# Forgetting attention: how the rows of maxima, the turned values, the keys' low parts and the gates' sum are made

## What is computed

```python
q, k, v, g, f_logit = jnp.split(h @ w_in, [1024, 2048, 3072, 4096], axis=-1)
log_f = jax.nn.log_sigmoid(f_logit + b_f)              # (S, 16)
qh, kh, vh = rms_norm(heads(q), q_gain), rms_norm(heads(k), k_gain), heads(v)
c = jnp.cumsum(log_f, axis=-1)                          # per head, over positions
logits = qh @ kh.T * scale + c[t] - c[s]                # causal: s <= t
o = softmax(logits) @ vh
out = (o * jax.nn.silu(g)) @ w_out
```

## Time and profile before

| | us |
|---|---|
| median of 3 runs (2279.71 to 2282.96) | 2281.61 |
| the profiled execution | 2281.86 |
| its span, first to last instruction | 2279.7 |
| PE busy in the span (96%) | 2180.8 |
| DVE busy (53%) | 1209.2 |
| ACT busy (38%) | 860.2 |
| POOL busy (24%) | 546.3 |

### The profile page before, as it was taken

How to read it: one execution, slowest core, us unless ns; L and a number is a source line. 1 busy time by engine, 2 the same in 40 slices (tenths; PEclk the granted TensorE clock), 3 DMA queues, 4 the chain that set the end, 5 groups by cost and what they waited for, 6 DMA issues and landing times.

```text
span 2279.7 us, 29292 instructions
## 1 busy us (share of the span) xinstructions
PE 2180.8 (96%) x11216; PEld 1847.7 (81%) x11216; DVE 1209.2 (53%) x1583; ACT 860.2 (38%) x1351; POOL 546.3 (24%) x292
## 2 busy tenths in 40 slices
PE   4899999999999899999899999999999999999997
PEld 4678888988888788898878877888888888878886
DVE  6963332352442634334254464566666666676745
ACT  3135554211012343323222234445546546544322
POOL 1322222333332122213223222211111111110520
PEclk9999999999999899999999999999999999999998
DMA  8112112111441211001141122111111111012201
GB/s 344 56 47 74 66 64 75 65 37 55 158 157 37 93 39 54 29 28 47 38 148 47 37 93 75 34 51 37 46 51 38 40 55 46 28 46 93 93 19 74
DMA packets 37814, 154.61 MB, mean 68 GB/s; under 512 B 4289, under 2 KB 4289, under 8 KB 36962
## 3 DMA queue, kind: packets, MB, share of 16 engines
q1 hardware_dynamic: 24992, 93.52, 11.6%
q10 hardware_dynamic: 12738, 59.87, 7.5%
HBM read 128.15 MB, written 21.04 MB: 65 GB/s over the span
## 4 chain that ended last, share of the span: by engine, by line
PE 85%; DVE 9%; issue 3%; ACT 2%; DMA 0%; DVEq 0%; SPq 0%; ACTq 0%
PE psG L322 22%; PE psG L323 21%; PE psG L324 21%; PE psA L2377 2%; PE psA L2359 2%; PE psA L2358 2%; PE psA L2375 2%; PE psA L2374 1%; PE psA L2231 1%; PE psA L322 1%; PE psA L2333 1%; PE psA L324 1%; PE psA L323 1%; DVE M L1044 1%; PE psA L422 1%
## 5 line engine op out<-in xcount | busy, mean ns | idle before, releaser
L322 PE MATMUL psG<-AH,WH 128*128 128x512 f32 x2092 | 849.5, 406 | 34.0 <-DVE AL L1000 12.2
L324 PE MATMUL psG<-AH,WL 128*128 128x512 f32 x2092 | 822.9, 393 | 0.0
L323 PE MATMUL psG<-AL,WH 128*128 128x512 f32 x2092 | 822.8, 393 | 0.0
L309 POOL TENSOR_SCALAR WH<-RAW 128x1024 fp32r<-128x1024 f32 x144 | 165.6, 1150 | 1655.7 <-PE psG L322 1148.8
L322 PEld LDWEIGHTS psG<-AH,WH 128*128 128x128 f32 x2092 | 397.6, 190 | 115.0 <-issue 23.0
L324 PEld LDWEIGHTS psG<-AH,WL 128*128 128x128 f32 x2092 | 396.6, 190 | 87.5
L323 PEld LDWEIGHTS psG<-AL,WH 128*128 128x128 f32 x2092 | 398.7, 191 | 67.6
L311 POOL TENSOR_TENSOR WL<-RAW,WH 128x1024 fp32r<-128x1024 f32 x144 | 380.8, 2645 | 12.0
L2658 DVE TENSOR_TENSOR FTL<-psA,FTH 128x512 fp32r<-128x512 f32 x192 | 106.9, 557 | 117.1 <-ACT FTH L2533 113.4
L2526 ACT ACTIVATE psA<-psA,PB 128x512 f32<-128x512 f32 x192 | 106.3, 553 | 90.4 <-PE psA L2361 53.4
L2668 DVE RECIPROCAL FDR<-psA 64x128 f32<-64x128 f32 x128 | 118.5, 941 | 33.8 <-PE psA L2377 30.9
(11 more groups left out here) (376 smaller groups left out, 3088.2 us busy)
## 6 DMA issues: line engine op xcount, KB each, us to landing
RAW<-w_tiles SPq DMA_DIRECT2D x144, 512.0 KB, 3.5
gates<-SIG ACTq DMA_DIRECT2D x16, 512.0 KB, 2.9
park<-X ACTq DMA_DIRECT2D x2, 4096.0 KB, 11.1
CB<-fox_c ACTq DMA_DIRECT2D x16, 512.0 KB, 4.3
X<-xT SPq DMA_DIRECT2D x4, 1024.0 KB, 12.1
WADA_SCALE<-w_ada SPq DMA_DIRECT2D x1, 4096.0 KB, 23.2
WADA_SHIFT<-w_ada SPq DMA_DIRECT2D x1, 4096.0 KB, 33.5
WADA_GATE<-w_ada ACTq DMA_DIRECT2D x1, 4096.0 KB, 16.4
```

Source lines behind the costliest of these rows:

```text
L309: nc.gpsimd.tensor_scalar(WH[:, i, :], RAW[:, i % RAW_SLOTS, :], 1.0, 0.0, ALU.mult, ALU.add).then_inc(w_high, 1)
L322: first = nc.tensor.matmul(out, wh, xh, start=start, stop=False)
L323: nc.tensor.matmul(out, wh, xl, start=False, stop=False)
L324: return first, nc.tensor.matmul(out, wl, xh, start=False, stop=stop)
```

## The change

1. **Gates.** LFT is laid out head by head (16 heads x 8 blocks = 128 columns), so that one matmul with `causal_sum` sums all blocks within themselves: 128 rows (head, block) by 128 positions. CF is now 128x128. Its last column times a new constant matrix `carry_sum` gives each row the total of the earlier blocks of its head; ACT adds it as a bias. One transpose of CF takes the place of eight, and the store to fox_c is 128 rows of 128. NCT and PB change their layout with it.
2. **First keys by halves.** The LO half of pair 0's key tile runs right behind the LO loop, in bank 3 of psA, and its HI half behind the HI loop, in bank 2. `pe_hi_sums` now stands behind the whole LO loop, `pe_hi_spread` behind the key's chunk 3. ACT takes the keys' raw values out of psA in four instructions of 512 columns, and does so behind the copy of the gates' sum.
3. **Maxima as eight rows.** `row(r)` is one transpose of NMX's eight columns into 8 rows of 128 (bank 3). ACT makes eight copies of 8x128, the n-th with column n of the identity as scale, so that row n keeps only its own block and the others become zero; FKB has eight rows of -1 (`max_rows`) that add them up. On ACT `row(1)` moves behind `high(1)`.
4. **Values behind row 6.** The first head's scores use the halves of psA in the other order, so pair(0) is free after row 6. The values are turned there, ahead of `row(0)`, in PE's order and in ACT's. Score 4 of the second head, no longer score 0, waits for ACT's `row(0)`.
5. **Keys' low parts among short rows.** `dve_fox_k` makes one half of one head: behind rows 1 and 2 of the first head, and behind rows 0 and 2 of the second. `turned(0)` waits for four of them.
6. The fill lists move one cut from the pieces to the maxima; the sums stay.

The layouts, `act_fox_raw` (taken out, now inline), the declarations and the memset of `max_rows` are left out here.

```diff
@@ -2098,9 +2100,9 @@
     SUMS_AT = HALF - 4 * NB
-    FILL_MAX = [0, 1, 1, 1, 1, 1, 1, 1, 2, 0, 1, 2, 1, 1, 1, 1, 1, 1, 2]
-    FILL_SUM = [3, 1, 1, 1, 1, 1, 1, 2, 1, 1, 1, 1, 2, 1, 1, 1, 1, 1, 1, 1, 1, 1, 1, 1]
-    FILL_MAX_LAST = [0, 0, 0, 0, 0, 0, 1, 1, 2, 0, 1, 2, 2, 1, 1, 2, 2, 2, 2]
+    FILL_MAX = [0, 1, 1, 1, 1, 1, 1, 1, 1, 2, 1, 2, 1, 1, 1, 1, 1, 1, 2]
+    FILL_SUM = [2, 1, 1, 1, 1, 1, 1, 2, 1, 1, 1, 1, 2, 1, 1, 1, 1, 1, 1, 1, 1, 1, 1, 1]
+    FILL_MAX_LAST = [0, 0, 0, 0, 0, 0, 1, 1, 1, 1, 1, 2, 2, 1, 1, 2, 2, 2, 2]
     FILL_SUM_LAST = [3, 1, 1, 1, 1, 1, 1, 1, 1, 1, 1, 1, 1, 1, 1, 1, 1, 1, 1, 1, 1, 1, 1, 1]
     def filled(n):
...
@@ -2154,8 +2156,8 @@
     def other_rows(r):
         return head_rows(1 - r)
-    def max_row(r):
-        return slice(64 * (1 - r), 64 * (1 - r) + 1)
+    def max_rows(r):
+        return slice(64 * (1 - r), 64 * (1 - r) + NB)
     def piece(j):
...
@@ -2268,11 +2270,17 @@
                         f.then_inc(tile_begun, 1)
                     if h and n == KC + lag - 1:
                         l.then_inc(psum_full, 1)
-                if h == 0 and n == 3:
-                    pe_hi_sums(pe, 4)
-                elif h == 0 and n == 6:
+
+            if h == 0:
+                pe_hi_sums(pe, 4)
+                pe.wait_ge(w_split, T_FOX + 2)
+            for c in range(KC):
+                f, l = half_cut(psA[:, 3 - h, :], (T_FOX + 1) % 4, c, cols)
+                if h == 0 and c == 3:
                     pe_hi_spread(pe, 4)
-        gemm(pe, *fox_tile(0, 1))
+                elif h and c == 0:
+                    f.then_inc(tile_begun, 1)
+        l.then_inc(psum_full, 1)
         pe.wait_ge(f_ready, 1)
         for n in range(NB):
...
@@ -2280,23 +2288,18 @@
                                     mat("ident")[0:FOX_HEADS, 0:FOX_HEADS])
         l.then_inc(f_turned, 1)
         pe.wait_ge(f_ready, 2)
-        for n in range(NB):
-            for m in range(n + 1):
-                l = nc.tensor.matmul(psA[0:FOX_HEADS, 2 + n // 4, (n % 4) * P:(n % 4 + 1) * P], LFT[:, m, :],
-                                     mat("causal_sum" if m == n else "ones"), start=(m == 0), stop=(m == n))
-        l.then_inc(f_turned, 1)
+        nc.tensor.matmul(psA[:, 1, 0:P], LFT[:, :, :].rearrange("p h n -> p (h n)"), mat("causal_sum"), start=True, stop=True).then_inc(f_turned, 1)
         v, gate = list(gemm_slices(pe, *fox_tile(0, 2))), list(gemm_slices(pe, *fox_tile(0, 3)))
         pe_fox_sums(pe, 0, 0)
-        for cut in v[:4]:
-            cut()
-        pe_fox_sums(pe, 0, 1)
-        for cut in v[4:6]:
+        for cut in v[:3]:
             cut()
         pe.wait_ge(f_high, 1)
-        for n in range(NB):
-            l = nc.tensor.transpose(psA[:, 2, n * FOX_HEADS:(n + 1) * FOX_HEADS], CF[0:FOX_HEADS, n * P:(n + 1) * P],
-                                    mat("ident")[0:FOX_HEADS, 0:FOX_HEADS])
-        l.then_inc(f_turned, 1)
+        nc.tensor.matmul(psA[:, 1, P:P + 1], mat("carry_sum"), CF[:, P - 1:P], start=True, stop=True).then_inc(f_turned, 1)
+        pe_fox_sums(pe, 0, 1)
+        for cut in v[3:6]:
+            cut()
+        pe.wait_ge(f_high, 2)
+        nc.tensor.transpose(psA[:, 2, 0:P], CF[:, :], mat("ident")).then_inc(f_turned, 1)
         pe_fox_spread(pe, 0, 0)
         for cut in v[6:12]:
             cut()
...
@@ -2338,10 +2341,7 @@
         def row(r):
             pe.wait_ge(fmax_ready, p * N_S + NB * (r + 1))
-            for n in range(NB):
-                l = nc.tensor.transpose(psA[:, 2 + n // 4, (n % 4) * P:(n % 4 + 1) * P],
-                                        NMX[:, r * NB + n:r * NB + n + 1].to_broadcast([P, P]), mat("ident"))
-            l.then_inc(fm_full, 1)
+            nc.tensor.transpose(psA[0:NB, 3, HALF - P:HALF], NMX[:, r * NB:(r + 1) * NB], mat("ident")).then_inc(fm_full, 1)
         def turned(j):
...
@@ -2381,27 +2381,28 @@
             if i == 0:
                 pe.wait_ge(fqk_ready, p * 2 + 1)
                 pe.wait_ge(fdup_ready, p * 2 + 1)
-            elif i == 1:
-                pe.wait_ge(fn_done, p * 2 + 2)
-            else:
+            elif i >= 2:
                 pe.wait_ge(fmax_ready, p * N_S + (i - 1))
-            score(i, 0, (i + 1) % 2)
+            score(i, 0, i % 2)
         fill(fill_max[NB])
-        row(0)
+        pe.wait_ge(fmax_ready, p * N_S + (NB - 1))
         pe.wait_ge(psum_free, p * 4 + (U_FOX + 3))
         for n in range(NB):
             l = nc.tensor.transpose(psA[:, n // 4, (n % 4) * P:(n % 4 + 1) * P], VF[:, n * P:(n + 1) * P], mat("ident"))
         l.then_inc(fv_turned, 1)
+        fill(fill_max[NB + 1])
+        row(0)
         for i in range(NB):
             fill(fill_max[NB + 2 + i])
             if i == 0:
                 pe.wait_ge(fqk_ready, p * 2 + 2)
                 pe.wait_ge(fdup_ready, p * 2 + 2)
-                pe.wait_ge(fm_ready, p * 2 + 1)
             elif i == 1:
                 pe.wait_ge(fv_ready, p + 1)
             else:
                 pe.wait_ge(fmax_ready, p * N_S + (NB + i - 1))
+            if i == 4:
+                pe.wait_ge(fm_ready, p * 2 + 1)
             score(i, 1, (i + 1) % 2)
         fill(fill_max[2 * NB + 2])
         row(1)
...
@@ -2497,15 +2492,26 @@
         nc.scalar.activation(EXF[fs, :], EXF[fs, :], ACT.Ln, bias=mat("ones")[fs, 0:1]).then_inc(f_log, 1)
         nc.scalar.activation(FHIDE[:, :], HIDE[:, 2, :].bitcast(F32), ACT.Copy, scale=-1.0)
         act.wait_ge(f_turned, 1)
-        act_fox_raw(act, 0, 0)
-        act_fox_raw(act, 0, 1)
+        act.wait_ge(psum_full, U_FOX + 1)
+        nc.scalar.activation(FSQ[0][:, :], fox_buf(0), ACT.Square).then_inc(fsq_ready, 1)
+        nc.scalar.activation(FN[0], fox_buf(0), ACT.Copy).then_inc(psum_free, 1)
         act.wait_ge(f_turned, 2)
-        nc.scalar.activation(CF[fs, :], pair(1)[fs, :], ACT.Copy).then_inc(f_high, 1)
-        act.wait_ge(f_high, 1)
-        act.dma_start(fox_c, CF[fs, :]).then_inc(c_stored, 16)
+        nc.scalar.activation(CF[:, :], psA[:, 1, 0:P], ACT.Copy).then_inc(f_high, 1)
+        act.wait_ge(psum_full, U_FOX + 2)
+        for h, cols in enumerate((LO, HI)):
+            l = nc.scalar.activation(FSQ[1][:, cols], psA[:, 3 - h, :], ACT.Square)
+        l.then_inc(fsq_ready, 1)
+        for h, cols in enumerate((LO, HI)):
+            l = nc.scalar.activation(FN[1][:, cols], psA[:, 3 - h, :], ACT.Copy)
+        l.then_inc(psum_free, 1)
+        act.wait_ge(f_turned, 3)
+        alink(nc.scalar.activation(CARRY[:, :], psA[:, 1, P:P + 1], ACT.Copy))
+        nc.scalar.activation(CF[:, :], CF[:, :], ACT.Identity, bias=CARRY[:, :]).then_inc(f_high, 1)
+        act.wait_ge(f_high, 2)
+        act.dma_start(fox_c.rearrange("h (n t) -> (h n) t", t=P), CF[:, :]).then_inc(c_stored, 16)
         act_fox_root(act, 0)
-        act.wait_ge(f_turned, 3)
-        nc.scalar.activation(NCT[:, :, :].rearrange("p n h -> p (n h)"), psA[:, 2, 0:NB * FOX_HEADS], ACT.Copy, scale=-1.0).then_inc(nct_ready, 1)
+        act.wait_ge(f_turned, 4)
+        nc.scalar.activation(NCT[:, :, :].rearrange("p h n -> p (h n)"), psA[:, 2, 0:NB * FOX_HEADS], ACT.Copy, scale=-1.0).then_inc(nct_ready, 1)
         act.wait_ge(c_stored, 16)
         for r in range(2):
             act_fox_c(act, 0, r)
...
@@ -2518,12 +2524,14 @@
         def row(r):
             act.wait_ge(fm_full, p * 2 + (r + 1))
-            nc.scalar.activation(FX2[max_row(r), r, :], pair(1)[max_row(r), :], ACT.Copy).then_inc(fm_ready, 1)
+            for n in range(NB):
+                l = nc.scalar.activation(FX2[max_rows(r), r, n * P:(n + 1) * P], psA[0:NB, 3, HALF - P:HALF], ACT.Copy, scale=mat("ident")[0:NB, n:n + 1])
+            l.then_inc(fm_ready, 1)
         def exp(j):
             r, h, n, lo, w = piece(j)
             act.wait_ge(ft_full, p * N_P + (j + 1))
-            nc.scalar.activation(psA[:, j % 2, 0:w], psA[:, j % 2, 0:w], ACT.Exp, bias=PB[:, n, r:r + 1], scale=-1.0).then_inc(fexp_done, 1)
+            nc.scalar.activation(psA[:, j % 2, 0:w], psA[:, j % 2, 0:w], ACT.Exp, bias=PB[:, r, n:n + 1], scale=-1.0).then_inc(fexp_done, 1)
         def high(j):
             r, h, n, lo, w = piece(j)
...
@@ -2543,18 +2551,19 @@
         if not more:
             act_fill(act, 7, Y[:, 2, :], (fo_read, 12), 2)
             act_fill(act, 7, Y[:, 3, :], (fo_read, 16), 3)
-        row(0)
         act.wait_ge(fv_turned, p + 1)
         for r in range(2):
             l = nc.scalar.activation(FVH[:, :, 2 * HD * r:2 * HD * r + HD], pair(0).rearrange("p (n f) -> p n f", f=P)[:, :, HD * r:HD * r + HD], ACT.Copy)
         l.then_inc(fv_high, 1)
+        row(0)
         if not more:
             for j in range(4, N_FOX_CUT):
                 act_fill(act, 7, Y[:, j, :], (fo_read, 4 * (j + 1)), j)
-        row(1)
         for j in range(N_P):
             exp(j)
             high(j)
+            if j == 1:
+                row(1)
             for x, at in enumerate((Q_AT, K_AT)):
                 if more and j in at:
```

(23 more changed lines are left out.)

18 lines of the change are left out of this document (7 added, 11 removed).

## The result

| | before | after |
|---|---|---|
| median of 5 runs | 2280.64 | 2264.55 us (2261.95 to 2269.72) |
| profiled execution, span | 2281.86, 2279.7 | 2264.58, 2262.8 |
| PE busy | 2180.8 | 2165.4 |

The ratio is 0.9928 (95% interval 0.9913 to 0.9943): faster by 0.7%, 16 us where 25.5 were forecast; 2264.55 lies inside the range of 2246 to 2270, 8.5 above the forecast of 2256.

The account below looks back on a forecast made before the run. PE bounds the kernel, busy 82.98 of each pair's 83.6 us, with longer waits in the join. Gains of 13.2 (join), 8.8 (seven looped pairs) and 3.5 (last pair) sum to 25.5 us: forecast 2256, range 2246 to 2270.

Parts of the forecast that it names:

- The hole: Join: closing PE's 4.98 us stand before the sums brings the gates' transposes 6.4 us earlier, with 1.8 new idle.
- One matmul for 36: Join, sum of the gates: 36 matmuls taking 8.03 us become one of 0.22; sums of squares start 13.7 earlier altogether.
- The clock in the join: Join: the new 1.8 us idle may drop the clock, costing up to 1.7 us; 0.5 taken.
- Removed from a pass: Each looped pair: 1.46 us of transposes removed and 0.9 of waits closed, a gain of 2.36.
- both opened waits: Each looped pair: new PE waits, 0.2 us for ACT's copies and 0.9 for DVE against POOL.
- DVE behind POOL: First head's short rows: POOL holds the second key half on DVE, so PE waits 0.9 us a pair at score 5.
- Rival A: Loop: DVE and POOL don't meet, +6.3; with the join's clock up, gain 32 to 34, 2248 us; chance 0.15.
- ACT's eight copies: Second head, before exp(2): eight scaled copies replace one, taken as 1.4 us; PE waits 0.2 a pair, 1.0 at 2.2.
- rival B: Loop: both opened waits at their far ends, 1.7 and 1.0 a pair; gain 14, 2267 us; chance 0.2.
- rival C: Loop: the 0.9 us wait brings the clock down in every pair; gain 13.5, 2268 us; chance 0.07.
- The last pair: Last pair: values' low parts made earlier and second row shortened; gain 3.5 us (2 to 5).

Follow-up runs that it names:

- gates36: The one matmul that sums the gates issued 36 times, all else as the changed kernel; 2271.51 us, 0.9954 of before.
- hole_open: Against the changed kernel, key's 16 cuts in one piece behind both loops, sums and spread back among the low halves; 2269.00 us, 0.9956 of before.
- gate_early: Against the changed kernel, three of the gate tile's cuts moved into the join's wait for DVE's log f; 2264.38 us, 0.9928 of before.
- best_cover: Changed kernel with keys' low parts in second head's rows, second head's maxima by DVE, cuts moved into the join's waits and sums; 2247.97 us, 0.9843 of before.
- k_second: Against the changed kernel, all four halves of the keys' low parts moved into the second head's rows; 2259.88 us, 0.9901 of before.

## Why the prediction was right, and where it was off

The direction and the range held. The median is 8.5 us above the forecast; in the profiled execution the parts are:

- **The hole** (gain 6.4 to the gates' transposes): the joins' 72.44 and 59.85 split at the transposes into 35.34 and 28.84, so 6.5. Right, with the wait of 1.75 that was forecast as 1.8.
- **One matmul for 36** (7.3 more to the sums): gates36 gives 7.0 without the clock. Right.
- **The clock in the join**, "I take 0.5", at most 1.7: the mis-sized term. It lost 1.7 here and 8.5 in four other traces of the same join. I priced one short stretch behind one wait. What I left out: the 36 matmuls were dense work in front of thin sums. Traces suggest that with them went what kept the clock up, but most rest on one trace of a kernel: before and hole_open, both without the wait of 1.75, have no fall and one of 3.4 us at the sums; behind the wait, 36 matmuls ended the fall after 6.8 us (gates36), while it lasted 17.1 in four traces with one matmul, but 3.4 in the two of after. The Trainium skill, TensorE: Matmul & The Clock Gate, section "A second HAM failure mode: psum-queue depth-cycling", says that short idle gaps between groups of matmuls can be enough; the fall of gate_early behind gaps of 0.38 and 0.24 agrees.
- **3.3 us ahead of the join**, in code that wasn't touched: not in the sum. It goes with more time at the lower level (half of it up to there is 29.0 us, against 21.2 before; a part falls into waits and costs nothing); why the clock fell more often is open.
- **Removed from a pass, 2.36**: best_cover, with both opened waits closed, has 2.43. Right.
- **DVE behind POOL, 0.9**: the row of 2.35 stands as worked through (first half in the gap, second held, score 5 late), and k_second prices it at 0.97. Rival A is out. The rule of the Trainium skill, SBUF — State Buffer, "Who interferes with whom", holds as an exclusive lock; its price without the gap (1.7) doesn't appear, since the first half kept its 0.68.
- **ACT's eight copies, 0.2**: mis-sized, measured 0.8. I took a pitch of 0.17 from rows 7; it was 0.26 (2.09 for the row, inside the 2.2 that I had as the other end, for which I had said 1.0). A copy of eight rows takes 0.34, one of 128 rows 0.28 (rows 7); that one has no scale of its own, and whether the scale or the repetition costs the rest isn't separated. This is 4.1 of the 5.0 us by which the loop fell short. Half of rival B came true.
- **The clock in the loop** (rival C): 1.00 with a wait of 0.79 in each pass. Out.
- **The last pair, 3.5**: 3.4 up to its first weighing (16.51 early there, 13.13 at its first score), 3.0 to its end. The size is right, the parts less so: before has two low stretches of 3.4 us in this pair and after has one, so 1.7 of the gain is the clock, which the sum left out. I had also read the slow transposes at 2031.67 as a consequence of the wait of 1.69. The clock was back at 1.00 from 2028.6 to 2031.7; they follow the wait of 1.84.

By these parts: 3.3 ahead, 0.6 in the join, 5.0 in the loop, 0.5 in the last pair, less 0.8 behind it, makes 8.6 in the profiled executions; the median is 8.5 off. More than half of the miss (5.0) is the loop, mostly by ACT's copies; the 3.3 ahead of the join is no term of the change, and could have fallen the other way.
